# Placing split weights and activations at other SBUF addresses modulo 512 bytes in a float32r decoder trunk

## The reference

```python
x = x + 0.5 * swiglu(rms_norm(x, ffn1_norm), w_gate1, w_up1, w_down1)
h = rms_norm(x, mix_norm)
qa, ka, va, c_q, c_kv, k_r, g_a, g_b = split(h @ w_in)
o_a = swa_attention(qa, ka, va, ...)        # 8 heads, window of 128
o_b = mla_attention(c_q, c_kv, k_r, ...)    # 8 heads, low-rank q and kv
merged = sigmoid(g_a) * (o_a @ w_branch_a) + sigmoid(g_b) * (o_b @ w_branch_b)
x = x + merged @ w_out
x = x + 0.5 * swiglu(rms_norm(x, ffn2_norm), w_gate2, w_up2, w_down2)
# swiglu(x, g, u, d) = (silu(x @ g) * (x @ u)) @ d
```

## Time and profile before

| | us |
|---|---|
| median of 3 runs | 1043.81 (1042.66 to 1044.01) |
| the profiled execution's own time | 1042.75 |
| its span, first to last instruction | 1041.0 |
| PE busy | 1036.3 |
| PEld busy | 896.0 |
| DVE busy | 718.0 |
| ACT busy | 585.8 |

### The profile page before, as it was taken

The page is one execution under the profiler, slowest core; times in us unless marked ns, Lnnn a source line. Parts: engine busy times, 40 slices in busy tenths (PEclk is TensorE's granted clock), DMA queues, the critical chain, the costliest instruction groups (busy, mean ns, idle before and its releaser), DMA issues.

```text
span 1041.0 us, 15559 instructions
## 1 busy us (share of the span) xinstructions
PE 1036.3 (100%) x5648; PEld 896.0 (86%) x5648; DVE 718.0 (69%) x1132; ACT 585.8 (56%) x935; POOL 62.0 (6%) x71
## 2 busy tenths in 40 slices
PE   9999999999999999999999999999999999999998
PEld 8888888998888888888888888889988888888887
DVE  7766676668786866666687666666688868676665
ACT  7545454557964655454565455455678646454552
POOL 0062000121100000000000000001211000000000
PEclk9999999999999999999999999999999999999999
DMA  7765554455335555555545555634454346545541
GB/s 267 257 228 178 201 166 161 145 188 195 132 122 202 182 194 177 211 184 204 182 150 198 197 198 180 210 132 154 150 203 162 122 162 223 201 164 199 192 171 61
DMA packets 35269, 187.53 MB, mean 180 GB/s; under 512 B 4368, under 2 KB 4384, under 8 KB 20128
## 3 DMA queue, kind: packets, MB, share of 16 engines
q1 hardware_dynamic: 34992, 186.51, 51.5%
q0 software_dynamic: 240, 0.53, 0.2%
HBM read 185.98 MB, written 1.05 MB: 180 GB/s over the span
## 4 chain that ended last, share of the span: by engine, by line
PE 99%; DMA 0%; ACT 0%; DVE 0%; issue 0%; ACTq 0%
PE ps L1365 96%; PE ps L1799 1%; PE ps L1389 1%; PE ps L1828 1%; DMA x_cols<-in_x_first 0%; PE ps L1864 0%; PE ps L1708 0%; PE ps L1700 0%; ACT hT L606 0%; PE ps L1410 0%; DVE x_cols L995 0%; ACT w_hi L550 0%; PE ps L1398 0%; ACTq L605 0%
## 5 line engine op out<-in xcount | busy, mean ns | idle before, releaser
L1365 PE MATMUL ps<-hT,w_hi 128*128 128x512 f32 x1408 | 340.9, 391 | 0.2 <-ACT w_hi L550 0.2
L1365 PEld LDWEIGHTS ps<-hT,w_hi 128*128 128x128 f32 x1408 | 259.4, 188 | 50.6 <-ACT w_hi L550 0.4
L880 DVE TENSOR_TENSOR w_lo<-w_raw,w_hi 128x2048 fp32r<-128x2048 f32 x82 | 188.0, 2293 | 87.3 <-ACT w_hi L545 87.3
L1365 PEld LDWEIGHTS ps<-hT,w_lo 128*128 128x128 f32 x1408 | 180.3, 191 | 7.0
L1365 PE MATMUL ps<-hT,w_lo 128*128 128x256 f32 x1408 | 182.3, 283 | 0.0
L1365 PE MATMUL ps<-w_hi,hT 128*128 128x512 f32 (+2 forms) x576 | 174.2, 377 | 0.0
L545 ACT ACTIVATE w_hi<-w_raw 128x2048 fp32r<-128x2048 f32 x85 | 162.0, 1905 | 13.4 <-PE ps L1365 13.2
L1365 PE MATMUL ps<-w_lo,aTh 128*128 128x512 f32 x352 | 137.2, 390 | 0.0
L1365 PE MATMUL ps<-w_hi,aTl 128*128 128x512 f32 x352 | 137.0, 389 | 0.0
L1365 PE MATMUL ps<-w_hi,aTh 128*128 128x512 f32 x352 | 136.8, 390 | 0.0
L574 ACT ACTIVATE S<-ps 128x256 f32<-128x256 f32 x88 | 33.6, 382 | 159.4 <-PE ps L1365 159.4
(11 more groups left out here) (168 smaller groups left out, 953.6 us busy)
## 6 DMA issues: line engine op xcount, KB each, us to landing
w_raw<-in_w_ffn SPq DMA_DIRECT2D x85, 1024.0 KB, 5.0
w_raw<-in_w_ffn SPq DMA_DIRECT2D x90, 512.0 KB, 5.7
w_raw<-in_w_gate SPq DMA_DIRECT2D x16, 1024.0 KB, 5.0
w_raw<-in_w_proj SPq DMA_DIRECT2D x16, 592.0 KB, 4.8
w_raw<-in_w_branch SPq DMA_DIRECT2D x8, 1024.0 KB, 4.8
w_raw<-in_w_out SPq DMA_DIRECT2D x8, 1024.0 KB, 4.8
w_raw<-in_w_uq SPq DMA_DIRECT2D x4, 384.0 KB, 3.0
w_raw<-in_w_ffn SPq DMA_DIRECT2D x4, 256.0 KB, 5.4
```

What stands on the lines that cost most here:

```text
L880: dve.tensor_tensor(wl_gu[b], raw_gu[b], wh_gu[b].bitcast(F32), ALU.subtract).then_inc(lo_gu.sem, 1)
L1365: return pe.matmul(dst, w, m, start=start, stop=stop, skip_group_check=True)
```

## The change

The high and low tiles get a slot length of 2176 columns (8704 bytes, a multiple of 512) in place of 2048, so that there is room to shift a block inside its slot. In the gate and up view, high parts lie 80 columns (320 bytes) into slot 0 and at the start of slot 1; low parts lie 80 columns into slot 0 and 120 columns (480 bytes) into slot 1. Down weights and the slots of the mixing block stay at the start of their slots. An unused tile of 48 columns (192 bytes) is put ahead of `aTh` and `aTl`, one of 8 columns (32 bytes) ahead of `oTh` and `oTl`.

```diff
+HI_SHIFT, LO_SHIFT = (80, 0), (80, 120)
+PART_SLOT = GU_COLS + 128
+AT_GAP, OT_GAP = 48, 8
         w_raw = sb("w_raw", [P, MIX_SLOTS * GU_COLS])
-        w_hi = sb("w_hi", [P, MIX_SLOTS * GU_COLS], F32R)
-        w_lo = sb("w_lo", [P, MIX_SLOTS * GU_COLS], F32R)
-        raw_gu, wh_gu, wl_gu = ([w[:, i * GU_COLS:(i + 1) * GU_COLS] for i in range(2)] for w in (w_raw, w_hi, w_lo))
-        raw_d, wh_d, wl_d = ([w[:, 2 * GU_COLS + i * DN_COLS:2 * GU_COLS + (i + 1) * DN_COLS] for i in range(2)]
-                             for w in (w_raw, w_hi, w_lo))
-        mix_raw, mix_hi, mix_lo = ([w[:, i * GU_COLS:(i + 1) * GU_COLS] for i in range(MIX_SLOTS)]
-                                   for w in (w_raw, w_hi, w_lo))
+        w_hi = sb("w_hi", [P, MIX_SLOTS * PART_SLOT], F32R)
+        w_lo = sb("w_lo", [P, MIX_SLOTS * PART_SLOT], F32R)
+        raw_gu = [w_raw[:, i * GU_COLS:(i + 1) * GU_COLS] for i in range(2)]
+        wh_gu, wl_gu = ([w[:, i * PART_SLOT + at:i * PART_SLOT + at + GU_COLS] for i, at in enumerate(shifts)]
+                        for w, shifts in ((w_hi, HI_SHIFT), (w_lo, LO_SHIFT)))
+        raw_d = [w_raw[:, 2 * GU_COLS + i * DN_COLS:2 * GU_COLS + (i + 1) * DN_COLS] for i in range(2)]
+        wh_d, wl_d = ([w[:, 2 * PART_SLOT + i * DN_COLS:2 * PART_SLOT + (i + 1) * DN_COLS] for i in range(2)]
+                      for w in (w_hi, w_lo))
+        mix_raw = [w_raw[:, i * GU_COLS:(i + 1) * GU_COLS] for i in range(MIX_SLOTS)]
+        mix_hi, mix_lo = ([w[:, i * PART_SLOT:i * PART_SLOT + GU_COLS] for i in range(MIX_SLOTS)] for w in (w_hi, w_lo))
         hT = sb("hT", [P, KC, 2, SEQ], F32R)
         hTh, hTl = hT[:, :, 0, :], hT[:, :, 1, :]
+        aT_gap = sb("aT_gap", [P, AT_GAP])
         aTh = sb("aTh", [P, 2, SEQ], F32R)
         aTl = sb("aTl", [P, 2, SEQ], F32R)
...
         S = sb("S", [P, HB, SEGS * P])
+        oT_gap = sb("oT_gap", [P, OT_GAP])
         oTh = sb("oTh", [P, 8, SEQ], F32R)
         oTl = sb("oTl", [P, 8, SEQ], F32R)
```

## The result

The changed kernel takes 1047.0 us (median of 6 runs, 1046.52 to 1047.58), the kernel before 1042.84 us (6 runs, 1042.66 to 1044.01). The ratio is 1.0037, with a 95% interval of 1.0027 to 1.0047. The change made the kernel 0.4% slower, where 0.8% faster was forecast. The profiled execution has a span of 1045.6 us, 4.6 more than before.

A forecast was written before the change was run, and what follows sets the result against it. PE was taken as the bound, through what each matmul costs it. The profiled 1042.75 us less 8.4 for low-weight matmuls, all else 0, made 1034.3; with 1.1 for the median, 1035.4 us, range 1022 to 1052.

The forecast's parts named there:

- What bounds the kernel: Whole kernel: PE busy 1036.3 of 1041.0 us, so only what each matmul costs PE sets the time.
- The loss is not fixed, and addresses move it: All matmuls: some 32 cycles lost each, varying 6 ns less to 7 ns more with where both operands read.
- Rival 2: All matmuls: the 32 cycles are a fixed cost of switching weights, addresses play no part; 1043.8 us, chance 0.14.
- Low weights, -6 ns each: Low gate and up matmuls of 256 columns: 1408 x 6 = 8.4 us less.
- 512-column streams at 0: High slot 0, down and attention: 2024 matmuls taken as unchanged, since no row falls below 389 to 390 ns.
- rival 3: Moved 512-column streams stay in a bad phase: 2024 x 5.3 = 10.7 us more, 1054.5 us, chance 0.22.
- its own point of decision, 4.2 ns: Moved 512-column streams: from 8.4 / 2024 = 4.2 ns a matmul on, rival 3 decides despite the low-weight gain.
- the prediction's own 2 us: Whole kernel: about 2 us, 0.2%, is what a measurement can tell.
- Passages of +0.03 us: Between feed-forward streams of different offsets: at most 176 x 0.03 = 5.3 us, taken as 0, kept for the range.
- Supply and unchanged stages: ACT and DVE keep up, 8.4 us over 88 blocks taking 0.1 us of cover each; projection, gates, output unchanged.

The follow-up runs named there:

- The kernel with everything moved: All shifts at 0, every tile from w_hi on 192 bytes further, address differences as in the kernel before: 1043.51 us, ratio to before 0.9997.
- the four single parts: Changed kernel with one part kept moved: low parts 1039.33 us, high parts of slot 0 1047.7, down activations 1045.42, attention outputs and low-rank vectors 1044.55.

## Why the prediction was wrong

**What bounds the kernel: right.** PE's busy time rose by 4.5 us and the time by 4.2. No wait changed by more than 0.2 us; the loss came from the pitches.

**The loss is not fixed, and addresses move it: right.** The kernel with everything moved, at 0.9997, and the four single parts show that it is the difference of the two addresses that acts. Rival 2, in which nothing moves, is out: the pitch of high parts went from 226.3 to 233.1 ns by an address alone. The prediction had drawn that rival also from two places of the Trainium skill ("SBUF — State Buffer", section "SBUF: two separate sides"; "TensorE: Matmul & The Clock Gate", section "Step-by-step: what each phase is for"). As far as they would have made the pitch independent of addresses, the traces don't agree; what inside PE or its memory makes the difference, they don't show.

**Low weights, -6 ns each: right in sign, 2.4 times too large.** They measured 2.5 ns (117.5 for 120.0), in all 3.4 us by the busy time where 8.4 was put. The 6 ns were read off the one matmul behind a change of stream. Such a state exists as a lasting one, at 113.3 ns, but neither slot 0 at 192, entered from high weights, nor slot 1 at 32, entered from low weights at 192, settled in it. This term was mis-sized by 5.0 us.

**512-column streams at 0: the step that failed.** "No row shows one below the usual 389 to 390 ns" was read as "they stay there". The same rows had 396 ns behind a change of stream and nothing below, so all the evidence of the trace lay on the slower side, and the edge of a one-sided range was taken for its middle. Put at 0, the term measured 7.3 us more: 4.0 for the high parts, 2.2 for down, 1.1 for attention. In the loop that is +6.8 ns a matmul on slot 0's high parts and +2.5 on down. This is the direction of rival 3, and for the high parts its mechanism too: their pitches of 231 and 236 ns are of the size that the kernel before shows only behind a change of stream, and here they last. Its size was less, 7.3 / 2024 = 3.6 ns in place of 5.3. That is under its own point of decision, 4.2 ns: had the low parts gained the 8.4 us, the kernel would have come out 1.1 us faster, which is no difference at the prediction's own 2 us. So the forecast of a faster kernel needed both terms to be wrong before it turned: the two are off by 7.3 + 5.0 = 12.3 us, and the profiled execution, at 1047.35 us, is 13.0 us over the forecast 1034.3.

**Passages of +0.03 us: rightly 0 here.** The unmoved high parts of slot 1 even gained, 3.64 us against 3.65. It is no rule: with both low slots at 320 the high parts behind them lost 0.7 us in all.

**Supply and unchanged stages: right.** No wait was added, ACT and DVE kept their times, and the projection and gate groups stayed as they were (384 matmuls with `hT` and the high weights last 395 ns before and after). The range held 1047.0, but the direction was the other one.

## What to carry to other kernels

Where PE is the bound, as here, and each matmul loads its weights beside a moving stream, measure the pitch (start to start) of each kind of matmul and each slot, and try the address difference of the two operands as a parameter, one kind at a time. A change that bundles several of them hides its good part: here one of four was worth -0.36% and the others +0.76% together. And when a trace shows a quantity scattering to one side of its usual value only, the usual value may be the edge of the range and not its middle, as it was for the 512-column streams here.

## What was not expected of the hardware

With gate and up weights, a float32r matmul of 512 columns and its weight load take 226.7 ns start to start at differences of 0 and 256 bytes, about 233 at 64, 128, 192, 384 and 448, and 228.8 at 320. Down, where the roles of the operands are exchanged, takes 229.2 at 192 and 448 and 233.3 at 320. One of 256 columns takes 120.0 at 0, and at 192, 320 and 448 it has two steady pitches, some 117.7 and some 113.3. Which of them it takes depends on the stream that it is entered from: with slot 1 at 320 in both kernels, slot 0 at 320 gave 117.7 and slot 0 at 0 gave 113.1. No engine's instructions differ between the two but in the address of slot 0's low parts. By what mechanism stream and load hinder each other stays open; the runs show only that the distance of their addresses and what runs ahead of the stream decide, not whether the two meet in a bank, a buffer or on a port. Nor was it tried whether the 512-column streams have a second, faster state at some difference when entered in another way.
